# Encoder trunk on one core: the first products by blocks of the inner dimension, and six constant products ahead of them

## The chip, the cores and the metric

The kernel runs on one core of a Trainium2 chip, in one launch. The metric is the device time of the launch in microseconds (us). The core has five engines that run side by side and meet at semaphores: TensorE (PE) multiplies, ScalarE (ACT) and VectorE (DVE) work elementwise, GpSimd (POOL) does small elementwise work and starts some transfers, SyncE (SP) starts the others. PSUM has eight banks, here `bank[0]` to `bank[7]`, of 128 x 512 float32 each; PE writes only there.

## What is computed

Two layers over a sequence of 512 tokens of width 1024, all float32. What matters here is the very start of the first layer, the product `x @ w_in`, and within that the columns of its second half `v`:

```python
def _chunked_spatial_gating(x, w_in, norm_g, norm_b, w_s, b_s, w_out):
    h = jax.nn.gelu(x @ w_in, approximate=False)      # (512 x 1024) @ (1024 x 4096)
    u, v = jnp.split(h, 2, axis=-1)
    v = _layer_norm(v, norm_g, norm_b)
    ...
    y = u * mixed.reshape(B, S, A_WIDTH)
    return y @ w_out
# layer 0: this mixer, layer 1: differential attention; each is followed by
# x = layer_norm(alpha * x + h), a gated MLP with a depthwise convolution, and layer_norm again
```

## The kernel before

**Split products.** Every float32 product is made of three products of type fp32r. Each operand is split into a high part (`w_hi`, `xt_hi`: a cast on ACT) and a low part (`w_lo`, `xt_lo`: the original less the high part, a subtraction on DVE), and PE adds high x high, high x low and low x high in one bank.

**Units.** Weights come in units of 128 x 2048 numbers (1 MB), numbered through the whole kernel. Unit u is loaded by SP to `w_raw[:, u % 2]`, cast by ACT to `w_hi`, and the rest taken by DVE (in places by POOL) to `w_lo`. SP starts the load of unit u when the semaphore `w_lo_done` has reached u - 1 (the slot of `w_raw` is then free), and ACT casts it when PE has raised `w_used` to u - 1 (the slot of `w_hi` is free). Each engine's program is written out by hand in a fixed order; an engine that waits holds up everything behind it.

**Group 0.** The first 512 columns of `v`, for all 512 tokens, need units 0 and 1: unit 0 is rows 0 to 511 of the weight (inner blocks k = 0 to 3, 128 rows each), unit 1 rows 512 to 1023 (k = 4 to 7). The tokens are four blocks t = 0 to 3 of 128, and block t sums up in `bank[t]`. PE needs x with the inner dimension across the partitions, so it transposes each 128 x 128 block of `x_tok` (`turn`, L1224) into banks 4 to 7, ACT casts it to `xt_hi`, DVE subtracts to `xt_lo`. Altogether group 0 is 32 transposes and 4 x 8 x 3 = 96 products of 128 x 512.

Before the change it goes by blocks of tokens: x is loaded in four loads of 128 tokens (`x_landed[t]`), units 0 and 1 in six pieces (`w_piece`, each cast by `piece` in ACT and finished by `piece` in DVE), and PE does token block 0 (`turn(0, 0)`, `first_rows(0)`: all of unit 0 for it), block 1, then unit 1 for both, then blocks 2 and 3:

```python
turn(0, 0)
first_rows(0)
first_rows(1)
unit_ready(1)
...
```

**What follows group 0.** PE transposes eight small matrices (L1380, after `setup_landed` from POOL's loads), then does group 1 with units 2 and 3; between the halves of group 1 stands `small_products` (L1389, L1393), which needs the gelu of all of group 0 (`v_act`) and two small DVE steps on `one_hot` (`dist_step`, L870 and L873). ACT's order there is: cast of the transposed small matrices (L512), cast of unit 3 (L431), the gelu of group 0 (L505). DVE's: unit 3's low part (L726), statistics of the gelu (L856), then `one_hot`. POOL waits for the last load of x (L1728) and then starts some fifteen small loads, and after `w_hi_done` 2 three large ones of constants (L1745, L1746).

The rest of the kernel, from group 1 to the last layer norm, is one long row of products with the loads running ahead of them, and the change doesn't touch it.

Of the kernel before, what the change touches and what calls it, by code (L numbers as in the profile page):

```python
# [17 lines left out]
P = 128  # L18
NB = 512
# [7 lines left out]
LN_EPS = 1e-5  # L27

# [17 lines left out]
def encoder_kernel(nc, x, positions, rel_bias_table, a_w_in, a_norm_g, a_norm_b, a_w_s, a_b_s,  # L46
# [3 lines left out]
    TB = S // P  # L50
# [146 lines left out]
    with ExitStack() as ctx:  # L197
# [9 lines left out]
        half_turned, half_hi, half_lo = sem("half_turned"), sem("half_hi"), sem("half_lo")  # L207
# [4 lines left out]
        x_landed = [sem(f"x_landed{t}") for t in range(TB)]  # L212
# [6 lines left out]
        pool_init, ident_done = sem("pool_init"), sem("ident_done")  # L219
# [59 lines left out]
        def turn_bank(e, t):  # L279

            return 4 + 2 * (t % 2) if e == 0 else 2 * t
# [18 lines left out]
        def _(sp):  # L300
# [53 lines left out]
            sp.dma_start(x_tok[:, 1, :], xv[1]).then_inc(x_landed[1], 16)  # L354
            for c in range(2):
                sp.dma_start(raw(1, NB)[:, 2 * c:2 * c + 2, :], cols(a_w_in[0], WIDTH, NB, 4 + 2 * c, 2)
                             ).then_inc(w_piece[4 + c], 16)
            for t in range(2, TB):
                sp.dma_start(x_tok[:, t, :], xv[t]).then_inc(x_landed[t], 16)
# [56 lines left out]
        def _(act_e):  # L416
# [16 lines left out]
            def split_rows(e, t):  # L433
                act_e.wait_ge(turned, TB * e + t + 1)
                for h in range(2):
                    ins = act_e.copy(xt_hi[:, 4 * h:4 * h + 4, t * P:t * P + P],  # L436
                                     bank[turn_bank(e, t) + h][:, :].rearrange("p (k n) -> p k n", n=P))
# [42 lines left out]
            def first_half(h):  # L480
                if h == 0:
                    act_e.wait_ge(half_turned, 1)
                else:
                    act_e.wait_ge(turned, 1)
                act_e.copy(xt_hi[:, 4 * h:4 * h + 4, 0:P], bank[4 + h][:, :].rearrange("p (k n) -> p k n", n=P)
                           ).then_inc(xt_hi_done if h else half_hi, 1)
# [8 lines left out]
            piece(4)  # L495
            piece(5)
            for t in range(2, TB):
                split_rows(0, t)
# [222 lines left out]
        def _(dve):  # L721
# [6 lines left out]
            def split_rows(e, t):  # L728
                dve.wait_ge(xt_hi_done, TB * e + t + 1)
                for h in range(2):  # L730
                    ins = dve.tensor_tensor(xt_lo[:, 4 * h:4 * h + 4, t * P:t * P + P],  # L731
                                            bank[turn_bank(e, t) + h][:, :].rearrange("p (k n) -> p k n", n=P),
# [102 lines left out]
            def first_half(h):  # L835
                if h == 0:
                    dve.wait_ge(half_hi, 1)
                else:
                    dve.wait_ge(xt_hi_done, 1)
                dve.tensor_tensor(xt_lo[:, 4 * h:4 * h + 4, 0:P], bank[4 + h][:, :].rearrange("p (k n) -> p k n", n=P),  # L840
                                  xt_hi[:, 4 * h:4 * h + 4, 0:P], ALU.subtract).then_inc(xt_lo_done if h else half_lo, 1)

            first_half(0)
            for p in range(4):
                piece(p)
            first_half(1)
            split_rows(0, 1)
            piece(4)
            piece(5)
            for t in range(2, TB):  # L850
                split_rows(0, t)
# [350 lines left out]
        def _(pe):  # L1202
# [11 lines left out]
            def turn(e, t):  # L1214

                if e == 0:
                    pe.wait_ge(x_landed[t], 16)
                    pe.wait_ge(ident_done, 1)
                else:
                    pe.wait_ge(rows_ready, TB * (e - 1) + t + 1)  # L1220
                if e == 0 and t >= 2:
                    pe.wait_ge(xt_lo_done, t - 1)
                for k in range(KD):
                    ins = pe.transpose(bank[turn_bank(e, t) + k // 4][:, k % 4 * P:k % 4 * P + P],  # L1224
                                       x_tok[:, t, k * P:k * P + P], ident[:, :])
                    if e == 0 and t == 0 and k == KD // 2 - 1:
                        ins.then_inc(half_turned, 1)
                    if k == 0 and t == 0 and e > 0:
# [26 lines left out]
            def tokens_first(e, u0, done):  # L1255

                unit_ready(u0)
                for t in range(TB):
                    pe.wait_ge(xt_lo_done, TB * e + t + 1)
# [74 lines left out]
            def first_rows(t):  # L1334
                hi = w_hi[:, 0, :].rearrange("p (k n) -> p k n", n=NB)
                lo = w_lo[:, 0, :].rearrange("p (k n) -> p k n", n=NB)
                cols = slice(t * P, t * P + P)
                if t == 0:
                    pe.wait_ge(half_hi, 1)
                else:  # L1340
                    pe.wait_ge(xt_hi_done, t + 1)
                for k in range(KD // 2):
                    if t == 0 and k < 3:
                        pe.wait_ge(piece_hi, k + 1)
                    elif t == 0:
                        pe.wait_ge(w_hi_done, 1)
                    pe.matmul(bank[t][:, :], xt_hi[:, k, cols], hi[:, k, :], start=k == 0, stop=False)
                for k in range(KD // 2):
# [498 lines left out]
```

## Time and profile before

| | |
|---|---|
| median of 3 runs | 1297.23 us (1295.92, 1297.23, and one at 2141.65) |
| the profiled execution | 1298.59 us |
| its span, first to last instruction | 1296.9 us |
| PE busy | 1277.5 us, 99% of the span |
| mean granted TensorE clock | 0.998 |
| group 0 over, PE starts on L1380 | 37.73 us from the span's start |
| bytes moved | 140.59 MB, mean 108 GB/s |

Times within the execution are microseconds from the start of its span; about 1.7 us of the execution lie outside the span. A "busy" matmul row runs from its start to its modelled end, and products overlap, so what a product costs is the distance between starts and not its own duration.

### The profile page before, as it was taken

To read this page: it belongs to the slowest core of one execution; us is meant where nothing else is said; L and a number is where in the kernel's file an instruction comes from. 1 tells how busy PE (TensorE), PEld (TensorE's weight loads), DVE (VectorE), ACT (ScalarE), POOL (GpSimd) and SP (SyncE) were. 2 spreads that over 40 slices of the span, in tenths; PEclk is the share of its full clock that TensorE was granted. 3 is DMA by queue.
4 is the path that set the end of the run, shared out by engine and by line. 5 is a ranking of instruction groups with operands and counts; after the bars stand their busy time and mean duration, and the time that the engine had idled before them with its cause. 6 is when DMAs were issued, how large, how long until landed. Compare 5 with 4: busy or idle time off the path is not lost.

```text
span 1296.9 us, 15592 instructions
## 1 busy us (share of the span) xinstructions
PE 1277.5 (99%) x6078; PEld 1051.6 (81%) x6078; DVE 637.2 (49%) x879; ACT 456.9 (35%) x545; POOL 154.6 (12%) x155
## 2 busy tenths in 40 slices
PE   7999999999999999999999999999999999999997
PEld 6788888889888888888888777787888888888886
DVE  3527868356443434433363566664743434343346
ACT  3522334322232323322314577766132323232230
POOL 3002000040000000000315443424200000000001
PEclk9999999999999999999999999999999999999999
DMA  8435932250323232222513334234122232322221
GB/s 271 134 98 134 241 126 86 97 195 1 128 86 103 84 105 84 103 96 94 185 48 99 98 90 122 81 115 141 55 98 97 95 99 90 103 90 102 95 103 65
DMA packets 99771, 140.59 MB, mean 108 GB/s; under 512 B 5200, under 2 KB 76968, under 8 KB 99472
## 3 DMA queue, kind: packets, MB, share of 16 engines
q1 hardware_dynamic: 94304, 127.67, 30.2%
q0 software_dynamic: 5280, 12.07, 3.6%
q8 instruction: 28, 0.46, 0.2%
q10 hardware_dynamic: 144, 0.26, 0.1%
q14 instruction: 15, 0.12, 0.0%
HBM read 137.85 MB, written 10.52 MB: 114 GB/s over the span
## 4 chain that ended last, share of the span: by engine, by line
PE 91%; DVE 4%; DMA 2%; issue 1%; ACT 1%; DVEq 0%; SPq 0%; ACTq 0%
PE bank L1208 30%; PE bank L1211 29%; PE bank L1212 29%; DMA w_raw<-in_a_w_in_dram 2%; PE bank L1570 1%; PE bank L1224 1%; DVE xt_lo L731 1%; PE bank L1594 1%; DVE x_tok L785 1%; DVE w_lo L726 1%; DVE r_stat L754 0%; ACT xt_hi L436 0%; DVE x_tok L748 0%; DVE x_tok L776 0%; PE bank L1430 0%
## 5 line engine op out<-in xcount | busy, mean ns | idle before, releaser
L1208 PE MATMUL bank<-xt_hi,w_hi 128*128 128x512 f32 (+1 forms) x1008 | 383.3, 380 | 1.9 <-DVE w_lo L726 1.5
L1212 PE MATMUL bank<-xt_hi,w_lo 128*128 128x512 f32 (+1 forms) x1008 | 378.9, 376 | 0.0
L1211 PE MATMUL bank<-xt_lo,w_hi 128*128 128x512 f32 (+1 forms) x1008 | 378.8, 376 | 0.0
L726 DVE TENSOR_TENSOR w_lo<-w_raw,w_hi 128x2048 fp32r<-128x2048 f32 x79 | 180.8, 2289 | 194.9 <-ACT w_hi L431 168.6
L1208 PEld LDWEIGHTS bank<-xt_hi,w_hi 128*128 128x128 f32 x1008 | 189.7, 188 | 38.3 <-issue 4.7
L1211 PEld LDWEIGHTS bank<-xt_lo,w_hi 128*128 128x128 f32 x1008 | 189.8, 188 | 34.9 <-issue 1.4
L1212 PEld LDWEIGHTS bank<-xt_hi,w_lo 128*128 128x128 f32 x1008 | 189.7, 188 | 34.8
L431 ACT CAST w_hi<-w_raw 128x2048 fp32r<-128x2048 f32 x53 | 101.3, 1912 | 198.7 <-PE bank L1208 188.4
L1208 PE MATMUL bank<-w_hi,s_hi 128*128 128x512 f32 x416 | 162.6, 391 | 0.0
L1211 PE MATMUL bank<-w_lo,s_hi 128*128 128x512 f32 x416 | 161.9, 389 | 0.0
L1212 PE MATMUL bank<-w_hi,s_lo 128*128 128x512 f32 x416 | 161.9, 389 | 0.0
L1789 POOL TENSOR_TENSOR w_lo<-w_raw,w_hi 128x512 fp32r<-128x512 f32 x64 | 81.8, 1310 | 511.2 <-ACT w_hi L431 495.8
L585 ACT CAST w_hi<-w_raw 128x2048 fp32r<-128x2048 f32 x42 | 80.1, 1907 | 134.4 <-PE bank L1208 134.4
L1010 DVE SCALAR_TENSOR_TENSOR conv<-bank,conv_p,conv 128x511 f32<-128x511 f32 x44 | 33.0, 750 | 147.3 <-ACT conv L572 147.3
L572 ACT ACTIVATE conv<-bank,conv_p 128x512 f32<-128x512 f32 x44 | 34.3, 779 | 176.0 <-PE bank L1212 176.0
L1208 PEld LDWEIGHTS bank<-w_hi,s_hi 128*128 128x128 f32 x416 | 78.1, 188 | 16.5 <-issue 0.2
L1211 PEld LDWEIGHTS bank<-w_lo,s_hi 128*128 128x128 f32 x416 | 78.1, 188 | 16.4 <-issue 0.2
L1212 PEld LDWEIGHTS bank<-w_hi,s_lo 128*128 128x128 f32 x416 | 78.1, 188 | 16.3
L1208 PE MATMUL bank<-w_hi,xt_hi 128*128 128x512 f32 (+1 forms) x216 | 78.7, 364 | 0.6 <-DVE w_lo L832 0.6
L1027 DVE TENSOR_TENSOR act<-conv,bank 128x512 f32 (+1 forms) x44 | 30.2, 687 | 98.9 <-PE bank L1212 98.9
L1212 PE MATMUL bank<-w_hi,xt_lo 128*128 128x512 f32 (+1 forms) x216 | 77.4, 358 | 0.0
L1211 PE MATMUL bank<-w_lo,xt_hi 128*128 128x512 f32 (+1 forms) x216 | 77.3, 358 | 0.0
(191 smaller groups left out, 1408.4 us busy)
## 6 DMA issues: line engine op xcount, KB each, us to landing
w_raw<-in_f_w_in_dram SPq DMA_DIRECT2D x44, 1024.0 KB, 5.1
w_raw<-in_f_w_down_dram SPq DMA_DIRECT2D x22, 1024.0 KB, 4.8
w_raw<-in_a_w_in_dram SPq DMA_DIRECT2D x14, 1024.0 KB, 5.6
bias_by_query_key<-bias_by_distance POOLq DMA_DIRECT2D x4, 2048.0 KB, 37.1
w_raw<-in_a_w_out_dram SPq DMA_DIRECT2D x8, 1024.0 KB, 4.8
w_raw<-in_b_w_qkv_dram SPq DMA_DIRECT2D x16, 512.0 KB, 5.1
bias_sb<-bias_by_query_key SPq DMA_DIRECT2D x32, 256.0 KB, 2.7
w_raw<-in_b_w_qkv_dram SPq DMA_DIRECT2D x4, 1024.0 KB, 5.2
```

The lines of the kernel that those rows point to most:

```text
L431: act_e.copy(hi_of(u), w_raw[:, u % 2, :]).then_inc(w_hi_done, 1)
L572: act_e.activation(conv[:, j, :], bank[j][:, :], ACT.Identity, bias=conv_col(l, NCP - 1, off + j), scale=conv_col(l, 1, off + j)).then_inc ...
L585: act_e.copy(w_hi[:, u % 2, :], w_raw[:, u % 2, :]).then_inc(w_hi_done, 1)
L726: dve.tensor_tensor(lo_of(u), w_raw[:, u % 2, :], hi_of(u), ALU.subtract).then_inc(w_lo_done, 1)
L731: ins = dve.tensor_tensor(xt_lo[:, 4 * h:4 * h + 4, t * P:t * P + P], bank[turn_bank(e, t) + h][:, :].rearrange("p (k n) -> p k n", n=P), ...
L785: return dve.scalar_tensor_tensor(out=x_tok[:, t, cols], in0=x_tok[:, t, cols], scalar=r_rs[:, t:t + 1], in1=ln_bc[:, 1, cols], op0=ALU.mu ...
L1010: dve.scalar_tensor_tensor(out=conv[:, j, 1:S], in0=bank[j][:, 0:S - 1], scalar=conv_p[:, l, bass.ds(off + j, 1)], in1=conv[:, j, 1:S], op ...
L1027: dve.tensor_tensor(dst, conv[:, j, :], bank[2 + j][:, :], ALU.mult).then_inc(act_done, 1)
L1208: ins = pe.matmul(o, a_hi, b_hi, start=start, stop=False)
L1211: pe.matmul(o, a_hi, b_lo, start=False, stop=False)
L1212: return pe.matmul(o, a_lo, b_hi, start=False, stop=stop)
L1789: ins = pool.tensor_tensor(lo_of(u)[:, part], w_raw[:, u % 2, part], hi_of(u)[:, part], ALU.subtract)
```

## The change

Group 0 now goes by blocks k of the inner dimension. x is loaded in five loads of columns, for all tokens at once (columns of k = 0, of k = 1, and of two k each for the rest), between the pieces of the weight. `turn_column(k)` transposes the four token blocks of one k into one bank (4 + k % 4), ACT casts that bank in one piece, DVE subtracts in one piece, and `column_product(k)` adds the twelve products of that k to banks 0 to 3. PE transposes two blocks ahead of the products. POOL fills `ones` first, raises the new semaphore `ones_made`, and PE multiplies `ones` by itself six times into bank 7 (128 x 128 x 128, float32, never read) before it waits for x. The later layers' `turn` and the counts of the semaphores `turned`, `xt_hi_done` and `xt_lo_done` are adapted (`row_count`); nothing else is moved.

```diff
-            xv = x[0].rearrange("(t p) d -> t p d", p=P)
-            sp.dma_start(x_tok[:, 0, :], xv[0]).then_inc(x_landed[0], 16)
-            for c in range(4):
+            xk = x[0].rearrange("(t p) d -> p t d", p=P)
+            def x_columns(c):
+                k = slice(X_COLS[c][0] * P, X_COLS[c][1] * P)
+                sp.dma_start(x_tok[:, :, k], xk[:, :, k]).then_inc(x_landed[c], 16)
...
+        X_COLS = [(0, 1), (1, 2), (2, 4), (4, 6), (6, 8)]
...
+            x_columns(0)
+            first_unit(0)
+            x_columns(1)
+            first_unit(1)
+            x_columns(2)
+            first_unit(2)
+            first_unit(3)
+            x_columns(3)
+            second_unit(0)
+            x_columns(4)
+            second_unit(1)
...
-            piece(0)
-            first_half(0)
-            piece(1)
-            piece(2)
-            piece(3)
-            first_half(1)
-            split_rows(0, 1)
-            piece(4)
-            piece(5)
-            for t in range(2, TB):
-                split_rows(0, t)
...
+            def turn_column(k):
+                pe.wait_ge(x_landed[[k0 <= k < k1 for k0, k1 in X_COLS].index(True)], 16)
+                if k == 0:
+                    pe.wait_ge(ident_done, 1)
+                if k >= 4:
+                    pe.wait_ge(xt_lo_done, k - 3)
+                for t in range(TB):
+                    ins = pe.transpose(col_bank(k)[:, t * P:t * P + P], x_tok[:, t, k * P:k * P + P], ident[:, :])
+                ins.then_inc(turned, 1)
...
+                hi_ready()
...
+                for t in range(TB):
+                    ins = hi_hi(t)
+                    if k == 4 and t == 0:
+                        ins.then_inc(w_used, 1)
+                w_lo_ready()
+                for t in range(TB):
+                    hi_lo(t)
+                pe.wait_ge(xt_lo_done, k + 1)
+                for t in range(TB):
+                    lo_hi(t)
+
+            pe.wait_ge(ones_made, 1)
+            for n in range(WARM_UP):
+                pe.matmul(bank[7][:, 0:P], ones[:, :], ones[:, :], start=True, stop=True)
+            turn_column(0)
+            turn_column(1)
+            for k in range(KD):
+                column_product(k)
+                if k + 2 < KD:
+                    turn_column(k + 2)
```

PE's order at the start of the program. Before (buffer numbers are kept: bank0 to bank3 are the sums of the four token blocks, L1224 the transposes, L1347 high x high, L1353 high x low, L1360 low x high):

```order
L1224 MATMUL bank4<-ident_103,x_tok_49 128x128 [waits ident_done,x_landed0]
L1224 MATMUL bank4<-ident_103,x_tok_49 128x128 x3
L1224 MATMUL bank5<-ident_103,x_tok_49 128x128 x4
L1347 MATMUL bank0<-w_hi_53,xt_hi_50 128x512 [waits piece_hi,half_hi]
L1347 MATMUL bank0<-w_hi_53,xt_hi_50 128x512 [waits piece_hi] x2
L1347 MATMUL bank0<-w_hi_53,xt_hi_50 128x512 [waits w_hi_done]
L1353 MATMUL bank0<-w_lo_54,xt_hi_50 128x512 [waits piece_lo] x3
L1353 MATMUL bank0<-w_lo_54,xt_hi_50 128x512 [waits w_lo_done]
L1224 MATMUL bank6<-ident_103,x_tok_49 128x128 [waits ident_done,x_landed1,half_lo]
```

And after (L1405 are the six constant products, L1349 the transposes, L1376, L1379 and L1382 the three kinds of product):

```order
L1405 MATMUL bank7<-ones_104 128x128 [waits ones_made]
L1405 MATMUL bank7<-ones_104 128x128 x5
L1349 MATMUL bank4<-ident_103,x_tok_49 128x128 [waits ident_done,x_landed0]
L1349 MATMUL bank4<-ident_103,x_tok_49 128x128 x3
L1349 MATMUL bank5<-ident_103,x_tok_49 128x128 [waits x_landed1]
L1349 MATMUL bank5<-ident_103,x_tok_49 128x128 x3
L1376 MATMUL bank0<-w_hi_53,xt_hi_50 128x512 [waits piece_hi,xt_hi_done]
L1376 MATMUL bank1<-w_hi_53,xt_hi_50 128x512
L1376 MATMUL bank2<-w_hi_53,xt_hi_50 128x512
L1376 MATMUL bank3<-w_hi_53,xt_hi_50 128x512
L1379 MATMUL bank0<-w_lo_54,xt_hi_50 128x512 [waits piece_lo]
```

Before, the first four products take four different pieces of the weight; now they take one piece and the four token blocks, and the second load of x stands ahead of them.

ACT's order at the same place, before:

```order
L477 CAST w_hi_53<-w_raw_52 128x512 [waits w_piece0]
L485 CAST xt_hi_50<-bank4 128x4x128 [waits half_turned]
L477 CAST w_hi_53<-w_raw_52 128x512 [waits w_piece1]
L477 CAST w_hi_53<-w_raw_52 128x512 [waits w_piece2]
L477 CAST w_hi_53<-w_raw_52 128x512 [waits w_piece3]
L485 CAST xt_hi_50<-bank5 128x4x128 [waits turned]
L436 CAST xt_hi_50<-bank6 128x4x128 [waits turned]
L436 CAST xt_hi_50<-bank7 128x4x128
L477 CAST w_hi_53<-w_raw_52 128x1024 [waits w_piece4]
L477 CAST w_hi_53<-w_raw_52 128x1024 [waits w_piece5]
```

And after, from the third column of x to the cast of unit 2:

```order
L497 CAST w_hi_53<-w_raw_52 128x512 [waits w_piece3]
L502 CAST xt_hi_50<-bank4 128x512 [waits turned]
L497 CAST w_hi_53<-w_raw_52 128x1024 [waits w_piece4]
L502 CAST xt_hi_50<-bank5 128x512 [waits turned]
L502 CAST xt_hi_50<-bank6 128x512 [waits turned]
L497 CAST w_hi_53<-w_raw_52 128x1024 [waits w_piece5]
L502 CAST xt_hi_50<-bank7 128x512 [waits turned]
L451 CAST w_hi_53<-w_raw_52 128x2048 [waits w_used,w_landed0]
```

The last piece of unit 1 (`w_piece5`) is now cast behind the column k = 6, which PE transposes after the products of k = 4; before, it stood ahead of the transposes of token blocks 2 and 3.

## Rows read from the trace of the kernel before

**Rows 1.** The page: busy share of PE, and the chain that ended last, by engine

```profile
PE 1277.5 (99%) x6078; PEld 1051.6 (81%) x6078; DVE 637.2 (49%) x879; ACT 456.9 (35%) x545; POOL 154.6 (12%) x155
...
PE 91%; DVE 4%; DMA 2%; issue 1%; ACT 1%; DVEq 0%; SPq 0%; ACTq 0%
```

**Rows 2.** Waits of PE: total us, times, longest us

```profile
PE bank L1224 <- DMA x_tok<-in_x_dram: 4.3, 1, 4.3
PE bank L1347 <- ACT w_hi L477: 1.8, 1, 1.8
```

**Rows 3.** Stretches of group 0 on PE: length, busy (instructions), clock, DMA share, GB/s

```profile
4.34:7.80 3.46, 3.28 (x10) 1.00 0.98 347
7.80:9.60 1.80, 0.00 (x2) 1.00 1.01 390
9.60:14.10 4.50, 4.50 (x14) 1.00 1.03 388
```

**Rows 4.** Timeline of PE in group 0: start, length, then what

```profile
4.34 1.97 PE L1224 MATMUL bank<-ident,x_tok 128*128 128x128 f32 x8 [4.34 <-DMA x_tok<-in_x_dram]
...
10.87 1.91 PE L1353 MATMUL bank<-w_lo,xt_hi 128*128 128x512 f32 x4
12.57 1.91 PE L1224 MATMUL bank<-ident,x_tok 128*128 128x128 f32 x8
...
16.67 1.09 PE L1353 MATMUL bank<-w_lo,xt_hi 128*128 128x512 f32 x4
17.60 1.07 PE L1360 MATMUL bank<-w_hi,xt_lo 128*128 128x512 f32 x4
```

**Rows 5.** The chain that ended last, from the end of group 0: start, length

```profile
37.73 0.87 PE bank L1380 x8
...
49.51 0.15 PE bank L1389 x2
49.66 1.81 PE bank L1393 x4
```

**Rows 6.** Timeline of the engines that start loads, and of the fill of `ones`

```profile
0.86 0.39 SPq L351 DMA_DIRECT2D x_tok<-in_x_dram  x1
...
1.03 0.20 POOL L1719 MEMSET ones<- 128x128 f32 x1
...
25.22 0.57 POOL L1745 DMA_DIRECT2D norm_bc<-in_a_norm_g_dram  x1
```

**Rows 7.** Single loads: KB, us from issue to landing

```profile
x_tok<-in_x_dram SPq DMA_DIRECT2D x1, 512.0 KB, 3.4
w_raw<-in_a_w_in_dram SPq DMA_DIRECT2D x1, 256.0 KB, 4.0
...
w_raw<-in_a_w_in_dram SPq DMA_DIRECT2D x1, 256.0 KB, 6.7
...
w_raw<-in_a_w_in_dram SPq DMA_DIRECT2D x1, 1024.0 KB, 6.2
...
norm_bc<-in_a_norm_g_dram POOLq DMA_DIRECT2D x1, 1024.0 KB, 8.0
norm_bc<-in_a_norm_b_dram POOLq DMA_DIRECT2D x1, 1024.0 KB, 9.3
...
bs_bc<-in_a_b_s_dram POOLq DMA_DIRECT2D x1, 512.0 KB, 10.7
```

**Rows 8.** Timeline of ACT and DVE: casts and subtractions of group 0, and `one_hot`

```profile
5.33 0.62 ACT L477 CAST w_hi<-w_raw 128x512 fp32r<-128x512 f32 x1 [3.18 <-DMA w_raw<-in_a_w_in_dram]
5.86 0.58 ACT L485 CAST xt_hi<-bank 128x512 fp32r<-128x512 f32 x1
...
15.48 2.02 ACT L477 CAST w_hi<-w_raw 128x1024 fp32r<-128x1024 f32 x2
...
6.47 0.69 DVE L840 TENSOR_TENSOR xt_lo<-bank,xt_hi 128x512 fp32r<-128x512 f32 x1 [6.47 <-ACT xt_hi L485]
...
16.83 2.35 DVE L832 TENSOR_TENSOR w_lo<-w_raw,w_hi 128x1024 fp32r<-128x1024 f32 x2
...
39.60 1.93 ACT L431 CAST w_hi<-w_raw 128x2048 fp32r<-128x2048 f32 x1
...
46.97 1.21 DVE L873 TENSOR_TENSOR one_hot<-one_hot,dist_row 32x1024 f32<-32x1024 f32 x1
```

**Rows 9.** Bytes moved, slices of 0.5 us from 740, over loads in 512-byte pieces

```profile
GB/s 66 180 279 0 0 8 53 365 321 346 347 265 289 317 304 52 3 0 0 0 0 0 0 0 0 0 0 0 131 209 184 0 0 0 12 193 295 25 0 0
```

More of the change, by code:

```diff
@@ L277, in rows_of, with col_bank, row_count @@
             return s_hi[:, j % 2, :, :], s_lo[:, j % 2, :, :]
[L279 to L281 removed]
+        def col_bank(k):
+            return bank[4 + k % 4]
+        def row_count(e, t):
+            return KD + TB * (e - 1) + t + 1
+        X_COLS = [(0, 1), (1, 2), (2, 4), (4, 6), (6, 8)]
         def gate_rows(m):
@@ L478, in piece, with column @@
                 ins.then_inc(w_hi_done if p in (3, 5) else piece_hi, 1)
[L480 to L486, printed above, removed]
+            def column(k):
+                act_e.wait_ge(turned, k + 1)
+                act_e.copy(xt_hi[:, k, :], col_bank(k)[:, :]).then_inc(xt_hi_done, 1)
             piece(0)
-            first_half(0)
+            column(0)
+            column(1)
             piece(1)
-            piece(2)
-            piece(3)
-            first_half(1)
-            split_rows(0, 1)
+            for k in range(2, 4):
+                column(k)
+                piece(k)
+            column(4)
             piece(4)
+            column(5)
+            column(6)
             piece(5)
-            for t in range(2, TB):
-                split_rows(0, t)
+            column(7)
             def token_group(g, i=None):
@@ L833, in piece, with column @@
                 ins.then_inc(w_lo_done if p in (3, 5) else piece_lo, 1)
[L835 to L847, printed above, removed]
+            def column(k):
+                dve.wait_ge(xt_hi_done, k + 1)
+                dve.tensor_tensor(xt_lo[:, k, :], col_bank(k)[:, :], xt_hi[:, k, :], ALU.subtract
+                                  ).then_inc(xt_lo_done, 1)
+            for k in range(4):
+                piece(k)
+                column(k)
             piece(4)
+            column(4)
+            column(5)
             piece(5)
-            for t in range(2, TB):
-                split_rows(0, t)
+            column(6)
+            column(7)
             def group_stats(g):
@@ L1331, in outward @@
                     out_unit(u0, n - 1, (3,), stop=True)
[L1334 to L1343, printed above, removed]
-                        pe.wait_ge(piece_hi, k + 1)
[L1345 to L1348, printed above, removed]
-                    if t == 0 and k < 3:
-                        pe.wait_ge(piece_lo, k + 1)
-                    elif t == 0:
-                        pe.wait_ge(w_lo_done, 1)
-                    pe.matmul(bank[t][:, :], xt_hi[:, k, cols], lo[:, k, :], start=False, stop=False)
-                if t == 0:
-                    pe.wait_ge(half_lo, 1)
-                    turn(0, 1)
-                else:
-                    pe.wait_ge(xt_lo_done, t + 1)
-                for k in range(KD // 2):
-                    pe.matmul(bank[t][:, :], xt_lo[:, k, cols], hi[:, k, :], start=False, stop=False)
```

92 lines of the change are left out of this document (49 added, 43 removed).

## The prediction

> **What bounds the kernel now.** I read the page's busy shares and its chain first, then PE's waits, then the stretches and the timeline of group 0, the only part that the change rewrites. PE is busy for 1277.5 of 1296.9 us and holds 91% of the chain that ended last [rows 1]. So each microsecond that group 0 ends earlier on PE is worth one at the end, as long as nothing behind it has to be waited for, and the most that there is to win lies between the span's start and 37.73, where PE starts on the eight transposes behind group 0 [rows 5].
>
> At full speed group 0 is little work. Four products start 0.93 us apart in all (16.67 to 17.60, so 0.23 each), and eight transposes hold 0.87 us of the chain, so 0.44 for four [rows 4, 5]. 96 x 0.23 + 8 x 0.44 = 21.9 + 3.5 = 25.4 us. The stage takes 37.73. The missing 12.3 us are: 4.3 waiting for x, then 1.8 for the third piece of the weight [rows 2]; some 1 us of smaller waits; and a slow start. Four products at 10.87 take 1.70 us until 12.57, which is 0.43 each: PE is then at the 1.2 GHz level, and at 16.67 at 2.4 GHz [rows 4]. The clock column reads 1.00 all along [rows 3], so at the start of the span only the distances tell. By them the level rose at about 14.1, in the transposes that began at 12.57, after PE had been busy without a break from 9.60; before that came the gap of 1.80 us and 3.46 us of transposes and products [rows 3]. Of 14.1 us PE worked 7.8 at half speed (3.28 + 4.50), which costs 3.9. 4.3 + 1.8 + 1 + 3.9 = 11.0; the remaining 1.3 I leave as hand-overs between engines.
>
> **The loads.** The total is the same 4 MB by SP in 11 starts for 10. Before, 0.52 MB of x had landed at 0.86 + 3.4 = 4.3, with the next 0.26 MB at 1.31 + 4.0 = 5.3 [rows 6, 7]. Now 0.26 MB of x come first and the weight's first piece second (0.52 MB together, so between 4.3 and 5), then k = 1 of x third (0.79 MB, 5.3 to 5.9). The loads for k = 0 and 1 are in pieces of 512 bytes; loads of that form elsewhere ran at 265 to 365 GB/s [rows 9] against 347 to 390 in group 0 [rows 3], on 0.5 MB a loss of 0.3 us at most. The load for k = 2 and 3 starts at about 2.65; a load that started at 2.24 took 6.7 us [rows 7], so it lands at about 9.5. From there the loads come faster than PE uses them: the last 2.6 MB need 7 us at 388 GB/s [rows 3], and PE needs 3.2 us for a k whose data is 0.5 MB.
>
> **The path to the first product.** PE transposes k = 0, then must wait for x of k = 1 and transpose that too, since both stand ahead of the products in its order. 5.4 for the landing, 0.9 for four transposes at the low level (eight took 1.97 at 4.34 [rows 4]): the first product starts at 6.4. Its other operands are there: the weight's first piece cast at 5.0 + 0.6, column 0 cast by ACT in 0.58, low parts by DVE in 0.69 each [rows 8], none later than 6.5 where the low parts are wanted a microsecond on.
>
> **The rest of group 0.** From 6.4 on PE has 96 products and six more turns: 6.4 + 21.9 + 2.6 = 30.9 at full speed. ACT needs 1.2 us per k and DVE 1.4 [rows 8], under half of PE's 3.2, and each column is cast while the products of the k before run (2.7 us), so they cost nothing once it runs; only a DVE or ACT step over twice as long would show.
>
> **The six constant products.** The nearest row is the two float32 products of 512 columns in `small_products` (the row counts four, two passes each) in 1.81 us [rows 5], so 0.9 each, and 0.23 for 128 columns at the high level, 0.45 at the low: 2.7 us for six. `ones` is now the first fill, ready near 1.1 instead of 1.23 [rows 6], so they end at 3.8, before or just as x lands. They cost nothing: what they may delay, the turn of k = 0, has to wait for x of k = 1 behind it. What they are worth is the level at which the first products run, and no row prices that, so from both sides. If they do nothing, the low level lasts from 6.4 as long as before from 9.60, to 10.9: 4.5 us at half speed lose 2.2. If PE is at the high level at 6.4, nothing is lost there, but the twelve products of k = 0 are over at 9.1 and PE waits for x of k = 2 until 9.5: 0.4. I take the middle, a rise within the products of k = 0, near 8: 1.8 us (6.4 to 8.2) at half speed lose 0.9, and the wait for x is covered. Group 0 ends at 30.9 + 0.9 = 31.8, 5.9 us earlier.
>
> **What is late next.** Unit 3's load waits for the low part of the last piece of unit 1. That piece is now cast behind column 6, so the low part is done about 8.7 - 1.0 - 2.0 = 5.7 us before group 0's end E (8.7 is PE's work behind the turn of k = 6; 0.6 + 1.0 on ACT, 1.2 on DVE [rows 8]), at 26, where before it was done at 19.2 and the load landed at 19.2 + 6.2 = 25.4 [rows 7, 8]. POOL's three large loads start in the same microseconds, as they did at 25.22 [rows 6], and took 8.0, 9.3 and 10.7 us beside each other [rows 7]. Unit 3's cast can start at E + 1.9 (39.60 - 37.73 [rows 5, 8]), and behind it hang gelu, statistics and `one_hot`, which was ready at 48.2 for a PE that came at 49.5 [rows 5, 8]: 1.3 us to spare. So a landing after E + 3.2 costs PE its excess. With 6.2 us it lands at E + 0.5 and costs nothing; with 10.7 at E + 5.0, which costs 1.8; with the middle one of the three, 9.3, at E + 3.6. I take that, 0.4 us, with 0 and 1.8 as the ends. The Trainium skill ("DMA: Bandwidth & Descriptors", section "Issuing engines are not separate DMA queues") says that loads from different engines run on the same 16 DMA engines and interleave. By it the 9.3 is the right neighbour, and without sharing the 6.2 would be and the term zero; the trace agrees so far as POOL's 512 KB load took 10.7 us in company.
>
> **Sum.** 5.9 - 0.4 = 5.5 us off. The profiled execution would go from 1298.59 to 1293.1, and the median, which stands 1.4 below it, from 1297.23 to **1291.7**. That is 0.4%; a difference of under 2% (26 us) is about what a measurement of this kernel can't tell from no change.
>
> **The rivals.**
>
> *The constant products do nothing for the clock.* Between them and the first product PE has only transposes and a wait. Then the low level lasts to 10.9, the products of k = 0 end at 11.3 instead of 9.1, and E = 30.9 + 2.2 = 33.1: 4.6 - 0.4 = 4.2 off, 1293.0. For it: the 3.46 us of work from 4.34 did not raise the level, and a gap of 1.80 followed [rows 3]. Against it: there was no constant work ahead of those. The Trainium skill ("TensorE: Matmul & The Clock Gate", "Part 4: PE-mode transpose") has a rule for this rival: transposes don't count as activity and the raised clock doesn't engage for them. By the rule the stretch from 3.8 to 6.4 would be idle for the clock. Half of it the trace refutes: eight transposes take 0.87 us at 37.73 and 1.97 at 4.34 [rows 4, 5], so they do run at both levels; whether they count no row shows.
>
> *The loads come late and the stage waits for them.* The three loads that landed within 4.1 us may have been those that began into empty queues; if x of k = 1, now the third, takes the 6.7 us of the fourth [rows 7], it lands at 8.5, the products start at 9.4, and with the 2.2 of the low level E = 36.1: 1.6 - 0.4 = 1.2 off, 1296.0. The change would then not do what it says, since PE would begin its products as late as before. For it: the jump from 4.1 to 6.7 within one row of equal loads. Against it: the same number of bytes is ahead of it as was ahead of a load that took 4.0.
>
> *Slower: unit 3 late.* The mechanism of the last term, priced at its worst. POOL's 2.6 MB took from 25.22 to 26.31 + 10.7 = 37.0 [rows 6, 7], 222 GB/s. If unit 3's 1 MB had to share that rate to the end, 3.7 MB take 16.5 us and it lands at 26.1 + 16.5 = 42.6 = E + 10.8, 7.6 over the limit: 5.9 - 7.6 = -1.7, 1298.9. It turns the change into a loss from a landing 15 us after its start. Against it: no load of the rows took more than 10.7.
>
> **How the numbers follow.** Forecast 0.60 (the level rises before or during the products of k = 0; E from 31.3 to 32.5, unit 3's term 0 to 1.8), the clock rival 0.25, late loads 0.08, unit 3 late 0.04, anything else 0.03. The forecast's own ends are 1290.8 and 1293.8; the clock rival reaches 1294.4 with the full 1.8 of unit 3. The runs of before lie 1.3 apart, so I add 1.3 on each side: 1289.5 to 1295.7. That leaves out most of the late loads and unit 3's worst. Chances: all cases lie within 2%, so 0.98 for no difference, and 0.01 each for the others.
>
> **What would show it.** In the new profile: PE's first product near 6.4, its last one of group 0 near 31.8; products of k = 0 that begin 0.43 apart and change to 0.23 within that k; a short wait or none at the transposes of k = 2; no wait of PE for ACT or DVE in k = 2 to 7; the w_raw load of unit 3 landing at 33 to 37, and at `small_products` a wait of PE of 0 to 1.8 us for DVE's `one_hot`. From there on everything shifted by the same 5.5 us, with PE's later waits unchanged. It is wrong if the first product starts after 8, if products at 0.43 go on beyond 11, if the wait at `small_products` is over 2 us, or if some later wait of PE grows by what was won.

## The result, and the profile after

The changed kernel takes 1301.3 us (median of 12 executions, 1298.7 to 1305.1) against 1296.9 us for the kernel before beside it: the ratio is 1.0038 [1.0027, 1.005], so it is 0.4% slower: clear of the noise, and within the 2% that the forecast expected with a chance of 0.98. One of the twelve executions of before took 2141.65 us and is not in the ratio. 1291.7 was forecast, in a range up to 1295.7. The forecast is wrong in its sign and in its range, although the stage that the change rewrites does almost exactly what was forecast of it.

The profiled execution of the changed kernel took 1298.72 us, with a span of 1297.1. That is its fastest of the twelve, which has to be kept in mind, while the profiled execution of before (1298.59, a span of 1296.9) lies 1.7 us above the median of before.

The page of the kernel after, PE's share and the chain by engine:

```profile
PE 1279.4 (99%) x6090; PEld 1053.2 (81%) x6090; DVE 637.9 (49%) x879; ACT 457.0 (35%) x545; POOL 154.9 (12%) x155
...
PE 84%; issue 7%; DVE 4%; DMA 4%; ACT 1%; POOL 0%; DVEq 0%; SPq 0%; ACTq 0%; POOLq 0%
```

Against [rows 1] PE is busy for 1.9 us more, and DMA has 4% of the chain instead of 2%: two weight loads of 20.5 and 25.5 us lie in it (units 11 and 13, below) where before had the second alone (25.7). The waits of PE (total us, times, longest us):

```profile
PE bank L1428 <- DVE one_hot L889: 2.3, 1, 2.3
PE bank L1349 <- DMA x_tok<-in_x_dram: 1.9, 1, 1.9
PE bank L1224 <- DVE w_lo L744: 1.4, 1, 1.4
PE bank L1405 <- POOL ones L1752: 1.1, 1, 1.1
```

The 4.3 us for x and the 1.8 us for the weight [rows 2] are gone, 1.9 us for x are left, and a new wait of 2.3 us for `one_hot` (L1428, L1393 before) is the longest of all. The opening on PE, and where group 0 ends (start, length):

```profile
1.12 2.93 PE L1405 MATMUL bank<-ones 128*128 128x128 f32 x12 [1.12 <-POOL ones L1752]
3.84 1.06 PE L1349 MATMUL bank<-ident,x_tok 128*128 128x128 f32 x4
6.81 0.66 PE L1349 MATMUL bank<-ident,x_tok 128*128 128x128 f32 x4 [1.91 <-DMA x_tok<-in_x_dram]
7.22 1.18 PE L1376 MATMUL bank<-w_hi,xt_hi 128*128 128x512 f32 x4
8.23 1.08 PE L1379 MATMUL bank<-w_lo,xt_hi 128*128 128x512 f32 x4
...
32.01 1.03 PE L1415 MATMUL bank<-ident,ws_raw 128*128 128x128 f32 x8
```

The first product starts at 7.22 and the next four at 8.23: 0.25 us each, the 2.4 GHz level from the first one on. Group 0 is over at 32.01, 5.7 us before the 37.73 of [rows 5].

Then unit 3. What its load, issued at 26.34, took from issue to landing (KB, us):

```profile
w_raw<-in_a_w_in_dram SPq DMA_DIRECT2D x1, 1024.0 KB, 11.4
```

And the timelines of SP, ACT, DVE and PE of the same execution, in order of time:

```profile
26.34 0.37 SPq L312 DMA_DIRECT2D w_raw<-in_a_w_in_dram  x1
...
37.73 1.91 ACT L451 CAST w_hi<-w_raw 128x2048 fp32r<-128x2048 f32 x1 [3.58 <-DMA w_raw<-in_a_w_in_dram]
...
45.09 1.21 DVE L889 TENSOR_TENSOR one_hot<-one_hot,dist_row 32x1024 f32<-32x1024 f32 x1
...
46.36 3.58 PE L1428 MATMUL bank<-one_hot,tab_sb 32*8 32x512 f32 x4 [2.26 <-DVE one_hot L889]
49.86 0.80 PE L1224 MATMUL bank<-w_hi,xt_hi 128*128 128x512 f32 x1
50.46 0.63 PE L1227 MATMUL bank<-w_lo,xt_hi 128*128 128x512 f32 x1
50.88 0.63 PE L1228 MATMUL bank<-w_hi,xt_lo 128*128 128x512 f32 x1
```

The load beside POOL's large ones took 11.4 us, its cast came at 37.73 instead of 33.9 (E + 1.9), `one_hot` was ready at 46.3, and PE had stood since 44.1. And then the products at L1428 take 3.5 us until the next start where [rows 5] had 1.81, and the ones behind stand 0.42 us apart. The stretches say the same by the clock. The columns are: length, busy of PE, of its weight loads, of DVE, ACT and POOL, then granted clock, DMA share and GB/s.

```profile
45.00:46.00 1.00, 0.00 (x0) 0.00 (x0) 0.97 (x2) 0.00 (x0) 0.00 (x0) 1.00 1.04 408
46.00:47.00 1.00, 0.64 (x1) 0.10 (x2) 1.00 (x4) 0.00 (x0) 0.00 (x0) 0.55 0.58 221
47.00:52.00 5.00, 5.00 (x9) 2.02 (x8) 1.77 (x8) 1.45 (x2) 0.00 (x0) 0.50 0.01 3
52.00:53.00 1.00, 1.00 (x4) 0.74 (x4) 0.32 (x1) 0.98 (x2) 0.00 (x0) 0.53 0.00 0
53.00:60.00 7.00, 7.00 (x32) 5.78 (x31) 4.77 (x7) 2.34 (x4) 0.00 (x0) 1.00 0.47 150
```

At the end of the wait the clock has fallen to 1.2 GHz and stays there until 53. Busy time times what the clock lacks to 1 is the lost work: 0.64 x 0.45 + 5.0 x 0.5 + 1.0 x 0.47 = 3.3 us. 5.7 won, less 2.3 of wait and 3.3 of clock: nothing is left at 53 us, and behind it the two profiles agree to within 0.2 us (the cast of unit 13, below, at 164.92 for 165.04).

What the profiles alone don't show is why the median is 4 us above before and not level with it. PE has one more wait, at L1224 for `w_lo` (L1208 before), far behind the change. Before, then after, the cast of that unit (13) on ACT, and what it stood for:

```profile
165.04 1.91 ACT L431 CAST w_hi<-w_raw 128x2048 fp32r<-128x2048 f32 x1 [6.00 <-DMA w_raw<-in_a_w_in_dram]
```

```profile
164.92 1.91 ACT L451 CAST w_hi<-w_raw 128x2048 fp32r<-128x2048 f32 x1 [5.97 <-DMA w_raw<-in_a_w_in_dram]
```

Its load was issued at 139.3 and took 25.7 us before and 25.5 after. Around it POOL copies the position bias, four transfers of 2 MB each, memory to memory, started back to back (L1764 before, L1799 after), and waits for their end. POOL's timeline of the kernel after shows it:

```profile
113.64 5.55 POOL L1799 DMA_DIRECT2D bias_by_query_key<-bias_by_distance  x4 [2.79 <-issue]
168.07 0.10 POOL L1811 MEMSET g_row<- 128x1 f32 x1 [48.88 <-DMA bias_by_query_key<-bias_by_distance]
```

8 MB of bias with four units of weights fill the DMA engines for 54 us, up to 168 (in the profile of before the DMA share is 0.90 to 1.07 in every stretch of 4 or 5 us from 116 to 165). Before, the same transfers ran from 114.71 to 168.03. This stretch moves less than PE does. In e3, below, PE comes 4.8 us earlier and the transfers begin at 108.91, 5.8 earlier, but they end at 166.47, only 1.6 earlier, and PE waits at the end. In the profiles of before and after both kernels had lost the difference by then, so both wait 1.4 to 1.5 us. That stretch was the suspect for the rest.

### The profile page after: what moved, and what is told of

It reads as the page before. It is cut to its first block, busy times and chain, and to the rows that moved or that the text cites. A ratio compares the mean times of both kernels' runs of the same rounds, so it can differ in the third digit from the quotient of the medians.

```text
span 1297.1 us, 15623 instructions
## 1 busy us (share of the span) xinstructions
PE 1279.4 (99%) x6090; PEld 1053.2 (81%) x6090; DVE 637.9 (49%) x879; ACT 457.0 (35%) x545; POOL 154.9 (12%) x155
## 4 chain that ended last, share of the span: by engine, by line
PE 84%; issue 7%; DVE 4%; DMA 4%; ACT 1%; POOL 0%; DVEq 0%; SPq 0%; ACTq 0%; POOLq 0%
PE bank L1224 27%; PE bank L1228 26%; PE bank L1227 26%; DMA w_raw<-in_a_w_in_dram 4%; PE bank L1605 1%; PE bank L1234 1%; DVE w_lo L744 1%; PE bank L1629 1%; DVE x_tok L803 1%; DVE xt_lo L749 0%; DVE r_stat L772 0%; DVE x_tok L766 0%; DMA x_tok<-in_x_dram 0%; PE bank L1376 0%; PE bank L1379 0%
## 5 line engine op out<-in xcount | busy, mean ns | idle before, releaser
L1224 PE MATMUL bank<-xt_hi,w_hi 128*128 128x512 f32 (+1 forms) x1008 | 383.4, 380 | 1.9 <-DVE w_lo L744 1.4
L1224 PEld LDWEIGHTS bank<-xt_hi,w_hi 128*128 128x128 f32 x1008 | 189.7, 188 | 38.2 <-issue 4.6
L1224 PE MATMUL bank<-w_hi,s_hi 128*128 128x512 f32 x416 | 162.6, 391 | 0.0
L1224 PEld LDWEIGHTS bank<-w_hi,s_hi 128*128 128x128 f32 x416 | 78.1, 188 | 16.6 <-issue 0.2
L1224 PE MATMUL bank<-w_hi,xt_hi 128*128 128x512 f32 (+1 forms) x192 | 69.7, 363 | 0.0
L1816 POOL TENSOR_TENSOR r_rs<-r_ve,neg_half 128x1 f32<-128x1 f32 x16 | 20.8, 1303 | 407.9 <-DVE r_ve L780 407.9
L1228 PE MATMUL bank<-w_hi,xt_lo 128*128 128x512 f32 (+1 forms) x192 | 68.5, 357 | 0.0
```

Source lines behind the costliest of these rows:

```text
L1224: ins = pe.matmul(o, a_hi, b_hi, start=start, stop=False)
L1228: return pe.matmul(o, a_lo, b_hi, start=False, stop=stop)
L1816: pool.tensor_tensor(r_rs[:, t:t + 1], r_ve[:, t:t + 1], neg_half[:, 0:1], ALU.pow).then_inc(rstd_done, 1)
```

## The experiments

All ratios are to the kernel before, measured beside each run on the same chip. The runs fall into four groups (e1 to e4, e5 to e8, e9 to e11, e12 to e14), on three chips, and the median of before was 1298.7, 1295.8, 1296.1 and 1296.0 us beside them, so across groups ratios are compared and not times.

**e1: the kernel after, once more, unchanged.**

> The changed kernel once more, for a second profile: its first one came from the fastest of its executions (1298.72 us, median 1301.3). Theory A (unit 3's load lands late, PE waits for one_hot at small_products, and in that wait its clock falls to the 1.2 GHz level): median 1299 to 1303; in the profile group 0 ends near 32 again, unit 3 lands between 36 and 42, and the wait at small_products and the stretch at the low level behind it differ from the first profile by what the span differs. Theory B (the block order costs somewhere else, in group 0's loads or behind group 1): group 0 ends later than 33, or some wait of PE behind 60 us is longer than before.

1.0051 [1.0033, 1.0069], median 1305.2, executions from 1297.9 to 1305.7. The loss is real. In its profile (the 1297.9) group 0 ends at 31.7 and the wait for `one_hot` is 2.0 us, but behind it the clock did not fall. The wait for `w_lo` is 2.9 us instead of 1.4, with the clock at 0.91 from 160 to 180.

**e2: the last piece of unit 1 one column earlier, on ACT and DVE**, so that unit 3's load starts earlier. ACT's part of the edit (DVE's is the same, with `piece(5)` ahead of `column(5)`):

```diff
             piece(4)
+            piece(5)
             column(5)
             column(6)
-            piece(5)
             column(7)
```

> Only change: the last piece of unit 1 is cast by ACT right behind piece 4 (ahead of columns 5 to 7), and its low part taken by DVE ahead of column 5, so that unit 3's load starts near 21.8 instead of 26.3. Theory A: unit 3 lands at 27 to 31, before PE needs it; no wait of PE at small_products, no fall of the clock there, and the 5.7 us of group 0 reach the end: 5 to 6.5 us under before, 1290 to 1292. Theory B: the wait at small_products goes but the time stays within 2 us of the changed kernel's, 1299 or more.

1.0006 [0.9994, 1.0018]. The wait for `one_hot` is gone, and the time is that of before: 0.45% less than e1, but not the 5 to 6.5 us below before that Theory A named. So the wait for `one_hot` was a cause, and not the only one. The load was issued at 24.5 and took 12.1 us, still beside POOL's. Group 0 ended only at 34.9, since PE began at 1.2 GHz here (below). The wait for `w_lo` is 2.9 us.

**e3: POOL's large loads wait until unit 3 has landed**, otherwise the kernel after.

```diff
             pool.wait_ge(w_hi_done, 2)
+            pool.wait_ge(w_landed[1], 16)
             for c, src in enumerate((a_norm_g, a_norm_b)):
```

> Only change: POOL starts its three large loads of constants only when unit 3 has landed. Unit 3's load still starts at 26.3. Theory A with sharing as the reason for its 11.4 us: it lands in 5.5 to 6.5 us, at 32 to 33, under the limit of E + 3.2 = 35.2; no wait at small_products, 1290 to 1293. If the sharing were not the reason (a load takes 11 us for another cause), it lands at 37 to 38 all the same and the time stays at 1299 to 1303. Theory B: no wait at small_products, time 1299 or more.

1.0006 [0.9994, 1.0019]. Unit 3's load, alone on the engines, takes 5.5 us instead of 11.4 and nothing waits at the small products; PE passes there 4.8 us ahead of the kernel before. So the sharing was the reason for the 11.4 us. And all of the lead is lost at 168 (PE's timeline):

```profile
167.77 0.79 PE L1224 MATMUL bank<-xt_hi,w_hi 128*128 128x512 f32 x1 [4.65 <-DVE w_lo L744]
168.36 0.63 PE L1227 MATMUL bank<-xt_lo,w_hi 128*128 128x512 f32 x1
```

Two stretches of the same execution, in the columns given above:

```profile
163.00:168.00 5.00, 0.35 (x3) 0.23 (x2) 2.65 (x3) 2.94 (x3) 0.10 (x1) 0.82 0.14 46
168.00:175.00 7.00, 7.00 (x21) 5.51 (x22) 6.70 (x15) 2.99 (x3) 0.00 (x0) 0.64 0.51 150
```

The wait for `w_lo` has grown from 1.5 to 4.65 us, and the clock falls in it: 7 x 0.36 = 2.5 us more. Here is the second place that takes back what the first leaves.

The chain that ended last names the transfers behind this wait. Before (start, length):

```profile
139.27 25.68 DMA w_raw<-in_a_w_in_dram
```

And in e3:

```profile
109.66 22.73 DMA w_raw<-in_a_w_in_dram
...
136.88 26.44 DMA w_raw<-in_a_w_in_dram
```

The second is unit 13's load, as before. The first is unit 11's, which took 5.8 us before. Here ACT and DVE have to wait for it (DVE 2.32 us), so unit 13's load, which needs unit 11's low part, starts 14.9 us behind unit 12's instead of 12.8.

**e4: twelve constant products on PE ahead of its wait for `one_hot`**, otherwise the kernel after. They compute nothing that is used.

```diff
+                for n in range(12):
+                    pe.matmul(bank[3][:, 0:P], ones[:, :], ones[:, :], start=True, stop=True)
                 pe.wait_ge(dist_step, 2)
```

> Only change: twelve constant products of 128 columns (2.7 us at 0.23 each) stand on PE ahead of its wait for one_hot in small_products. Unit 3 is as late as ever, so the place costs the same wait, but PE is not idle in it. Theory A says that of the loss at this place (about 2.3 us of wait, 1.7 us in the two products at half speed, 1.4 us in the products behind) only the wait is left: the clock stays at 2.4 GHz, 3 us less than the changed kernel, 1297 to 1299. If the clock's fall is no cause but an accompaniment, the time stays at 1301 or rises by up to 0.5.

1.0023 [1.001, 1.0036], between e1 and e2: 0.28% under e1 (3.2 us by the medians, where Theory A expected 3), though the two intervals just overlap. The clock stays at 2.4 GHz behind the small products. At 168 there is a wait of 3.5 us, with the clock at 0.91 from 160 to 180.

**e5: e2 and e3 together, and the bias transfers begin only when unit 11 has landed.** In the kernel before, POOL starts them 0.25 us behind that load, which takes 5.8 us; in the changed kernel 0.7 us ahead of it, and it takes 20.5. e5 asks whether that order is what costs.

```diff
                 for t in range(TB):
+                    if t == 0:
+                        pool.wait_ge(w_landed[1], 16 * 5)
                     ...
```

> The changed kernel with the last piece of unit 1 early (as in e2), POOL's three loads of constants behind unit 3 (as in e3), and POOL's four transfers of the bias table (2 MB each, memory to memory, near 110 to 168 us) started only when unit 11's load has landed. Theory C (the profiles of e1 to e4 gave rise to it): the four transfers fill the DMA engines for about 50 us; where they start before unit 11's load instead of behind it, that load takes 20 us instead of 6, the loads behind it start later, and PE's wait for unit 13 near 165 us grows from 1.5 to 2.9 or 4.6, with a fall of its clock in it. By C in this narrow form the wait goes back to about 1.5 and the time falls to 4 to 6 under before. If the order is not what matters but only the bytes (C wide: the end of the burst hardly moves when PE comes earlier), the wait stays at 3 to 5 and the time within 1.5 of before.

1.0007 [0.9996, 1.0017]. Unit 11 took 5.5 us, but unit 13, issued at 133.5, took 28.2, and PE waits 4.0 us. Unit 11 is waited for no longer, and PE's wait stays all the same: the order is at most a small part of it. What is left is the burst as a whole, and e6 takes it apart with the same bytes.

**e6: e2 and e3 together, and each bias transfer waits for one unit of weights** (units 11, 12, 13 and 14), so that the four are spread over the stretch.

```diff
                 for t in range(TB):
+                    pool.wait_ge(w_landed[1 - t % 2], 16 * (5 + (t + 1) // 2))
```

> As e5, but each of the four bias transfers waits for one more unit's load (units 11, 12, 13, 14), so that no load meets more than one of them. Both forms of theory C: no load takes over 14 us, no wait of PE near 165, and all of group 0's gain reaches the end, with the 1.5 us of the wait before on top: 6 to 8 us under before. If the gain of group 0 is lost somewhere else, less than 2 under before.

**0.9976 [0.9968, 0.9985]**, median 1292.9. Units 12 and 13 take 11.1 and 14.6 us instead of 18 to 28, and the wait for `w_lo` is gone. This is faster than both kernels. It is 2.9 us under before by the medians, where 6 to 8 were expected; e8 shows why.

**e7: the kernel after with the same spreading and nothing else. e8: the kernel before with it.**

> The changed kernel as it is, with only the spread bias transfers. Theory C with A: the wait near 165 is gone, the wait at small_products (2 to 2.3 us, and up to 3 more by the clock) stays: 2 to 5 us under before. If the loss of the changed kernel is all at small_products (A alone), it stays over before by 2 or more.

> The kernel before with only the spread bias transfers: what the burst costs without the change. Theory C: the wait of 1.5 near 165 goes, and with it the executions in which it was longer: 1.5 to 4 us under before, and its runs lie closer together. The difference between this one and e6 is then what the change is worth where nothing takes it back: 4.5 to 6 us.

e7: 1.0008 [0.9999, 1.0018]; e8: 1.0000 [0.9991, 1.0008]. So the spreading is worth nothing that can be told to the kernel before (1.5 to 4 us were expected) and 0.3 to 0.4% to the kernel after (1.0038 and 1.0051 without it, in other groups of runs). It is no gain of its own: it lets a gain through. What e7 lacks against e6 is the wait for `one_hot`, 2.3 us in its profile, with the clock at 0.77 from 46 to 52. In e8's profile group 0 ends at 35.5 and not at 37.7: the wait of 1.8 us for the third piece of the weight [rows 2] is not there.

**e9: e6 without the six constant products. e10: e6 once more. e11: e8 with the six constant products ahead of its first transposes.**

```diff
-WARM_UP = 6
+WARM_UP = 0
```

> The kernel of e6 (pieces one column earlier on both engines, POOL's large loads behind unit 3, each bias transfer behind a unit's load) without the six constant products; POOL's fill stays. What the six are worth is not known yet: group 0 ended anywhere from 31.3 to 34.9 us with them. Theory K (they raise the clock before the first product): without them the products stand 0.43 us apart at first and change to 0.23 some 4 to 5 us after the first one, group 0 ends 2 us later than with them, and the time is 1.5 to 2.5 us above e10's. Rival N (the clock at the start falls out one way or the other whatever ran before): the first products are as mixed as with them, and the time is within 0.7 us of e10's.

> The kernel of e6 once more, unchanged, so that the two beside it have it on their chip. Under either theory: 2 to 3.5 us below the kernel before, no wait for w_lo near 165, and a group 0 that ends at 31.5 to 34.

> The kernel before with POOL's bias transfers spread as in e8, and with the six constant products of the change ahead of its first transposes, nothing else of the change. Theory K: its transposes at 4.3 and the products at 5.9 run at the high level, eight transposes in 0.9 instead of 2 us, and group 0 ends up to 3.5 us earlier than the 35.4 to 37.7 of the kernels without; the gap for the third piece of the weight grows by what was won before it, so in the time 1 to 2.5 us below the kernel before. Rival N: group 0 ends at 35 to 38 and the time is that of the kernel before, within 0.7 us.

e9: 0.9975 [0.9966, 0.9983], 1292.97 us; e10: 0.9972 [0.9961, 0.9983], 1292.81 us. The six products are worth 0.2 us, which is nothing that can be told. In both profiles the first products of k = 0 are at 1.2 GHz. PE's timeline of e9, then of e10:

```profile
6.58 1.12 PE L1349 MATMUL bank<-ident,x_tok 128*128 128x128 f32 x4 [1.72 <-DMA x_tok<-in_x_dram]
7.35 2.05 PE L1376 MATMUL bank<-w_hi,xt_hi 128*128 128x512 f32 x4
9.20 1.91 PE L1379 MATMUL bank<-w_lo,xt_hi 128*128 128x512 f32 x4
10.91 1.27 PE L1382 MATMUL bank<-w_hi,xt_lo 128*128 128x512 f32 x4
```

```profile
1.12 2.93 PE L1405 MATMUL bank<-ones 128*128 128x128 f32 x12 [1.12 <-POOL ones L1752]
3.84 1.06 PE L1349 MATMUL bank<-ident,x_tok 128*128 128x128 f32 x4
6.64 1.11 PE L1349 MATMUL bank<-ident,x_tok 128*128 128x128 f32 x4 [1.74 <-DMA x_tok<-in_x_dram]
7.41 2.06 PE L1376 MATMUL bank<-w_hi,xt_hi 128*128 128x512 f32 x4
9.26 1.71 PE L1379 MATMUL bank<-w_lo,xt_hi 128*128 128x512 f32 x4
```

e11: 0.9988 [0.9979, 0.9997]. Its products are at 1.2 GHz until about 14, and its group 0 ends at 35.9, as late as e8's 35.5: the profile speaks for the rival, that the products do nothing. The ratio is 0.12% under e8's, in another group of runs and with overlapping intervals; whether the six do something there stays open.

**e12: the kernel after with the spreading of e7 and the twelve constant products of e4.**

> The kernel after the change, with the bias transfers spread as in e7 and the twelve constant products of e4 ahead of PE's wait for one_hot; pieces and POOL's large loads as the change has them. The wait of 2 us at the small products stays in length, but PE is busy in most of it. Theory F (what e7 lacks against e6 is the low clock that the wait sets off): the level stays at 2.4 GHz behind the wait, the mean clock of all executions is 0.998 and the time 1 to 2.5 us below e7's 0.9 above the kernel before, so 0.5 to 2 below it. Rival W (it is the wait itself, 2 us, that takes the gain): the time stays at 0 to 1 us above the kernel before.

0.9986 [0.9975, 0.9997], with a mean clock of 0.998 or more in ten of twelve executions, where ten of e7's eleven have 0.994 to 0.997. Against e7 that is 0.22%, 2.8 us by the ratios and 1.7 us by the medians against before beside each: the size of the clock loss, which is 1.7 us in e7's one profile. The wait itself is still there, filled with products. So a good part of what the wait costs is the clock behind it. PE's timeline of e12:

```profile
44.64 2.88 PE L1427 MATMUL bank<-ones 128*128 128x128 f32 x24
47.44 1.88 PE L1430 MATMUL bank<-one_hot,tab_sb 32*8 32x512 f32 x4
```

**e13, e14: the kernel after, one more profiled execution each.**

> The kernel after the change, one more execution with its profile. Its executions run from 1297.9 to 1305.7 us, and both profiles so far are of the fastest, with mean clocks of 0.995 and 0.997 where the slow ones have 0.991 to 0.994. Theory D (clock falls in the two waits): an execution of 1303 us or more shows over 8 us more at 1.2 GHz than the profiles so far, behind the waits at 44 and 168 us, and the waits themselves differ by under 2 us. Rival: the excess is a longer wait, 4 us and more, at full clock.

> The kernel after the change once more, for another draw. Theory D and its rival expect of it what they expect of e13: with a slow execution either more time at 1.2 GHz behind the two waits, or a longer wait at full clock.

1297.7 and 1298.7 us: no execution of 1303 us or more was caught, so Theory D and its rival are both undecided. Both show what the first profile shows: group 0 over at 32.0 and 32.1, 2.0 and 2.3 us of wait for `one_hot` with a clock of 0.83 from 40 to 60, and 0.8 and 1.5 us for `w_lo`.

**One account of all profiles.** Take off each span the moment at which group 0 ended, and what is left is the rest of the kernel. "Lost to clock" is, over one-microsecond stretches from 40 to 60 and 160 to 185, PE's busy time times what the granted clock lacks to 1.

| kernel | span | group 0 ends | rest | waits one_hot + w_lo | lost to clock |
|---|---|---|---|---|---|
| e10 | 1291.5 | 33.7 | 1257.8 | 0 + 0 | 0 |
| e9 | 1291.5 | 34.0 | 1257.5 | 0 + 0 | 0 |
| e6 | 1292.0 | 34.0 | 1258.0 | 0 + 0 | 0 |
| e8 | 1293.2 | 35.5 | 1257.8 | 0 + 0 | 0 |
| e11 | 1293.8 | 35.9 | 1257.9 | 0 + 0 | 0 |
| before | 1296.9 | 37.6 | 1259.3 | 0 + 1.5 | 0 |
| e2 | 1295.6 | 34.9 | 1260.7 | 0 + 2.9 | 0 |
| e7 | 1293.8 | 32.0 | 1261.8 | 2.3 + 0 | 1.7 |
| e3 | 1297.8 | 32.8 | 1265.0 | 0 + 4.6 | 2.6 |
| e1 | 1296.2 | 31.7 | 1264.5 | 2.0 + 2.9 | 1.7 |
| after | 1297.1 | 32.0 | 1265.1 | 2.3 + 1.4 | 3.3 |

In the five without a wait the rest is 1257.5 to 1258.0. In each of the others it is 1257.8 plus the waits plus the lost clock, to within 0.3 us (the 37.6 of before is PE's timeline; the chain has the same row at 37.73). e13 and e14 fit as well, and e5 to within 0.4. (e12 has 2.6 over, the 2.8 us of its twelve products. e4 has 8.0 over: 2.8 of its products, 3.5 of wait and 1.7 of clock.)

## Why the prediction was wrong, step by step

- **Group 0.** First product forecast at 6.4, measured 7.22: x of k = 1, issued at 1.90, took 4.9 us instead of 3.5. End forecast at 31.8, measured 32.0. That is luck in part: the start was 0.8 late, and no time was lost to the clock where 0.9 was put. (96 x 0.23 is 22.1 and not 21.9; from 7.22 to 32.01 the products and six turns took 24.8 us where 24.5 stood.)
- **The clock at the start.** "A rise within the products of k = 0" was the middle of two ends, and both ends occur. Of twelve profiles with the six constant products and the new order, seven were at 2.4 GHz through k = 0 (after, e1, e4, e5, e7, e13, e14), and five did it wholly or in part at 1.2 GHz (e2, e3, e6, e10, e12), ending group 0 at 32.7 to 34.9. In the time the six are worth 0.2 us, e9 against e10, as the rival had it that gave them nothing (0.25). That they may raise the level in some executions is left open: without them there is one profile of the new order.
- **"What there is to win."** 37.7 us was taken for the end of group 0 from the one profile of before. e8 and e11, with the same order of blocks, have 35.5 and 35.9, without the wait of 1.8 us for the third piece. Some 2 of the 5.7 us were that execution's and not the kernel's; where nothing takes the gain back, it is 0.24 to 0.28% (e6, e9, e10 against e8's 1.0000), 3.1 to 3.6 us and not 5.5.
- **Unit 3's term: the mechanism right, the size wrong.** It was priced at 0.4 us, with 0 and 1.8 as its ends, from a landing after 9.3 us. It took 11.4, beyond the highest row that was used (10.7), issued at 26.3 as forecast. The wait was 2.3 us; by the prediction's own limit of E + 3.2 a landing at E + 5.7 costs 2.5. The longest row, 10.7, would have been nearer than the middle one. The Trainium skill ("DMA: Bandwidth & Descriptors", section "Issuing engines are not separate DMA queues") says that loads from different engines interleave on the same 16 engines. The runs agree: the load took 5.5 us alone (e3) and 11.4 in company (the kernel after).
- **The wait was priced as a wait.** The 3.3 us of half clock behind it stood in no term, though the text had worked out that the low clock at the start of the span cost 3.9 us. This alone is larger than all that was put on unit 3.
- **The step that failed.** In the sum it is the term of 0.4 us for unit 3: with the clock in it, it measured 2.3 + 3.3 = 5.6 us in the profile after, and that takes back all but 0.1 of the 5.7. Behind the sum it is "From there on everything shifted by the same 5.5 us, with PE's later waits unchanged". The condition "as long as nothing behind it has to be waited for" was stated and then not looked up. PE's wait for `w_lo` near 169 stood in the trace of before with 1.5 us, in a stretch where unit 13 took 25.7 us to land, so "no load of the rows took more than 10.7" held for the rows and not for the trace. Where PE comes there earlier than before, in e3, e5 and e2, the wait grows to 4.6, 4.0 and 2.9 us, and in the longer two the clock falls in it. Why the burst ends so little earlier when it begins earlier is shown only in part, by unit 11's long load in e3. The prediction's sign of being wrong, "some later wait of PE grows by what was won", named the case; it got no chance.
- **The median.** The profiles account for executions of 1297.7 to 1298.7 us, and the two medians lie 2.6 and 7.4 us above the profiled execution beside them. The edits show where that goes: without the wait for `one_hot` the ratio falls by 0.45% (e2, e3 against e1), without the one for `w_lo` by 0.3 to 0.4% (e7), and without both by 0.6 to 0.8% (e6, e10). Whether the waits or the stretches at 1.2 GHz behind them grow in the longer executions stays open. In e1 the six executions at 1303.2 to 1305.7 have a mean clock of 0.9928 on average, against 0.997 in its profile: 0.0042 x 1304 = 5.5 us, most of the 7.4 us between median and profile. But among the first twelve the one of 1305.08 us and the profiled one of 1298.72 both have 0.995, so there the mean clock explains nothing of 6.4 us. No execution above 1299 us of this kernel has a profile.
- **The likeliest case held 0.60, and all slower ones 0.04.** The slower rival had the right transfer, but a price from which only a landing after 15 us gave a loss. With the clock in it, a landing after 11.4 us was enough for no gain.

## What to carry to other kernels

Before a microsecond won early is booked at the end, go through every later wait of the bounding engine in the trace, however short, and ask what sets its end: a wait for an engine that moves along shifts with the gain, but a wait at the end of a stretch full of DMA traffic can eat it. Price a new wait of TensorE as the wait plus the low clock that may follow it: here 2.3 us were followed by a loss of 1.7 to 3.3. And spread large background transfers over the loads that they compete with: 8 MB in one burst made a 1 MB load take 25 us, 8 MB in four parts 15. With that and with the wait for `one_hot` gone too, the gain of the change came through (0.9976, 0.9972 and, without the constant products, 0.9975). And before a gap in one profile is booked as what there is to win, see whether a second execution has it.

## What the runs showed of the hardware

- A wait of PE of 2.3 us, after steady work at 2.4 GHz, was followed by nearly 7 us at 1.2 GHz (granted clock 0.55, 0.50 and 0.53 in the stretches from 46 to 53). A wait of 2.0 us was followed by no fall in one execution (e1) and by a clock of 0.83 over 40 to 60 in another (e13); waits of 2.9 us at 168 had no fall in e2 and 0.91 over 160 to 180 in e1. The same program gives either.
- Six constant float32 products (two passes each, 2.7 us at 1.2 GHz: 0.23 per pass, against 0.12 in the fill of e12) ahead of a gap did not set the level of the first real products: in twelve profiles of kernels that have them and the new order it was high in seven and low, at least for a part, in five.
- Twelve constant products over a wait did keep the level, in both kernels that had them (e4, e12).
- One 1 MB load took 5.5 us alone, 11.4 to 12.1 beside the 2.6 MB that POOL had started, and beside 8 MB of memory-to-memory copies 16 to 28: the longest of the four, unit 13's, 24.3 to 28.2.
